# Reordered mixing stages, gate products moved into two projection units, and identity products between the steps of an encoder kernel

## What is computed

```python
def token_mixer(h, w_in, w_out, ...):
    proj = h @ w_in                                   # 1024 x 3088: 12 units of 256 or 512 columns and 16 gate columns
    p_ret, p_s5, p_hy, p_ml = jnp.split(proj, ...)
    y = jnp.concatenate([
        retention_mixer(p_ret, ...),   # rotary, 4 heads: scores * decay, then values, head norm
        s5_mixer(p_s5, ...),           # 16 groups of 64 complex states, forward and backward scan, GELU, gate
        hyena_mixer(p_hy, ...),        # short convolution, filters computed from w1..w3, 2 long convolutions by DFT
        mlstm_mixer(p_ml, ...)], -1)   # 4 heads, exponential gates, forward and backward, head norm
    return y @ w_out

def reference(x, ...):
    h = layer_norm(x, ...)
    for l in range(2):
        h = layer_norm(ALPHA * h + token_mixer(h, ...), ...)
        f = swiglu(h, ...) if l == 0 else moe_swiglu(h, ...)
        h = layer_norm(ALPHA * h + f, ...)
    return h
```

## Time and profile before

| | |
|---|---|
| median of 3 runs | 1711.05 us (1709.68 to 1712.01) |
| the profiled execution | 1715.15 us, its span 1713.3 us |
| mean granted clock of PE | 0.966 |
| busy: PE, DVE, ACT, POOL | 96%, 79%, 55%, 3% of the span |
| mixing stage 0 | 18.9 to 241.4 us |
| dense | 241.4 to 474.2 us |
| mixing stage 1 | 474.2 to 665.4 us |
| experts | 665.4 to 1713.3 us |

### The profile page before, as it was taken

How to read it: one execution, slowest core, us unless ns; L and a number is a source line. 1 busy time by engine, 2 the same in 40 slices (tenths; PEclk the granted TensorE clock), 3 DMA queues, 4 the chain that set the end, 5 groups by cost and what they waited for, 6 DMA issues and landing times.

```text
span 1713.3 us, 18404 instructions
## 1 busy us (share of the span) xinstructions
PE 1638.6 (96%) x7538; PEld 1278.9 (75%) x7538; DVE 1353.3 (79%) x1443; ACT 943.4 (55%) x941; POOL 56.5 (3%) x39
## 2 busy tenths in 40 slices
PE   6998989999999998899999999999999999999995
PEld 4555748988757665788888888888888888888883
DVE  6979456765666945688898888988989989888996
ACT  4312415644211231577776777777767767777772
POOL 0111000000011100000000000000000000000000
PEclk9999989999999988899999999999999999999997
DMA  7221152744433125598998998989989989989870
GB/s 313 98 98 49 74 213 98 271 172 154 185 134 142 49 81 240 200 377 340 370 355 344 368 359 339 360 347 360 365 347 356 360 339 369 362 329 374 351 300 26
DMA packets 40458, 444.21 MB, mean 259 GB/s; under 512 B 4400, under 2 KB 4528, under 8 KB 7216
## 3 DMA queue, kind: packets, MB, share of 16 engines
q1 hardware_dynamic: 39216, 438.78, 65.8%
q10 hardware_dynamic: 1152, 4.19, 0.6%
HBM read 437.71 MB, written 5.24 MB: 259 GB/s over the span
## 4 chain that ended last, share of the span: by engine, by line
PE 84%; DVE 11%; ACT 3%; issue 1%; DMA 0%; DVEq 0%; SPq 0%; ACTq 0%
PE bank L1062 34%; PE bank L1083 15%; PE bank L968 7%; PE bank L582 4%; PE bank L977 3%; PE bank L789 3%; PE bank L586 3%; PE bank L1026 2%; PE bank L1070 1%; PE bank L751 1%; DVE ring_lo L1943 1%; DVE ring_lo L2067 1%; ACT ex_up_hi L1334 1%; PE bank L1046 1%; PE bank L725 1%
## 5 line engine op out<-in xcount | busy, mean ns | idle before, releaser
L1943 DVE TENSOR_TENSOR ring_lo<-ring,ex_up_hi 128x2048 fp32r<-128x2048 f32 x224 | 513.0, 2290 | 50.9 <-ACT ex_up_hi L1334 50.7
L1334 ACT ACTIVATE ex_up_hi<-ring 128x2048 fp32r<-128x2048 f32 x224 | 429.1, 1916 | 115.9 <-PE bank L1062 108.2
L1062 PE MATMUL bank<-ex_up_hi,ex_x_hi 128*128 128x512 f32 x896 | 363.1, 405 | 3.7 <-DVE ring_lo L1943 3.7
L1062 PE MATMUL bank<-ring_lo,ex_x_hi 128*128 128x512 f32 x896 | 350.6, 391 | 0.0
L1062 PE MATMUL bank<-ex_up_hi,ex_x_lo 128*128 128x512 f32 x896 | 349.9, 390 | 0.0
L2067 DVE TENSOR_TENSOR ring_lo<-ring,ex_w_hi 128x2048 fp32r<-128x2048 f32 x112 | 255.6, 2282 | 1.4 <-ACT ex_w_hi L1430 1.4
L1430 ACT ACTIVATE ex_w_hi<-ring 128x2048 fp32r<-128x2048 f32 x112 | 213.2, 1904 | 0.0
L1062 PEld LDWEIGHTS bank<-ex_up_hi,ex_x_hi 128*128 128x128 f32 x896 | 168.3, 188 | 41.0 <-DVE ring_lo L1943 11.0
L1062 PEld LDWEIGHTS bank<-ring_lo,ex_x_hi 128*128 128x128 f32 x896 | 168.2, 188 | 36.1
L1062 PEld LDWEIGHTS bank<-ex_up_hi,ex_x_lo 128*128 128x128 f32 x896 | 168.8, 188 | 30.5
L1083 PE MATMUL bank<-ex_w_hi,ex_mid_hi 128*128 128x512 f32 x448 | 174.4, 389 | 2.1 <-DVE ex_mid_lo L2061 2.1
(11 more groups left out here) (313 smaller groups left out, 2140.5 us busy)
## 6 DMA issues: line engine op xcount, KB each, us to landing
ring<-moe SPq DMA_DIRECT2D x112, 2048.0 KB, 7.6
ring<-moe SPq DMA_DIRECT2D x112, 1024.0 KB, 7.4
ring<-ffn SPq DMA_DIRECT2D x11, 3072.0 KB, 10.9
win<-w_in SPq DMA_DIRECT2D x12, 2048.0 KB, 8.3
win<-w_out SPq DMA_DIRECT2D x4, 2048.0 KB, 10.3
lnb<-ln SPq DMA_DIRECT2D x4, 1024.0 KB, 6.6
tab<-yT ACTq DMA_DIRECT2D x8, 512.0 KB, 5.3
pr<-par SPq DMA_DIRECT2D x2, 1728.0 KB, 11.7
```

The lines of the kernel that those rows point to most:

```text
L1062: ins = mm(b[:, :], ex_x[x % 2][x_][:, k, :], (ex_up_hi, lo)[w_][:, k, :], start=(k == 0 and m == 0), stop=(k == KT - 1 and m == 2))
L1334: act(ex_up_hi[:, HS * q:HS * (q + 1), :], wt[:, HS * q:HS * (q + 1), :], ACT.Copy).then_inc(e_uh, 1)
L1943: tt(ring_lo[s][:, half], ring[s][:, half], hi.bitcast(F32), ALU.subtract).then_inc(e_ul, 1)
```

## The change

1. The gate products lose their unit. `unit` issues them for i = 8 and 9, one before each wide product on the same tokens, into bank 4 (columns 0 to 31). `UNITS` and `UNIT_BANK` have twelve entries, `pj` counts twelve units a layer, and `gates` waits for unit 9 and reads bank 4. In layer 1 unit 8 waits for one more spectrum to leave bank 4.
2. A new step on PE, `keep_busy(count, b)`: `count` products of the identity with itself, 128 x 128, into columns 384 to 511 of a bank; nothing reads them. They wait for nothing. Five calls in stage 0 (40 products), ten in stage 1 (68).
3. The lists `mix_0` and `mix_1` of PE, ACT and DVE stand in another order. No other piece of work is added or left out, and the lists of SP and POOL are the same but for the count of `pj`.

```diff
@@ -48,9 +48,9 @@
-UNITS = (0, 8, 9, 10, 11, 1, 2, 3, 12, 6, 7, 4, 5)
+UNITS = (0, 8, 9, 10, 11, 1, 2, 3, 6, 7, 4, 5)
...
-UNIT_BANK = (5, 6, 5, 6, 5, 6, 5, 6, 5, 6, 5, 1, 2)
+UNIT_BANK = (5, 6, 5, 6, 5, 6, 5, 6, 5, 6, 1, 2)
...
+            def keep_busy(count, b):
+
+                for _ in range(count):
+                    mm(bank[b][:, 384:512], ident, ident, start=True, stop=True)
...
-                elif i < 12:
+                else:
+                    with_gates = i in (8, 9)
+                    gw = W("gate_w").rearrange("p (k n) -> p k n", k=KT)
+                    if with_gates:
+                        pe.wait_ge(s_par, 16 * (l + 1))
+                        if l:
+                            pe.wait_ge(f_spec, 4 * l + 3)
                     for k in range(KT):
-                        ins = mm(b[:, :], hT[:, k, part * P:(part + 1) * P], w[:, k, :],
-                                 start=(k == 0), stop=(k == KT - 1))
-                else:
-                    gw = W("gate_w").rearrange("p (k n) -> p k n", k=KT)
-                    for t in range(TT):
-                        for k in range(KT):
-                            ins = mm(b[:, t * 16:(t + 1) * 16], hT[:, k, t * P:(t + 1) * P], gw[:, k, :],
-                                     start=(k == 0), stop=(k == KT - 1))
+                        x = hT[:, k, part * P:(part + 1) * P]
+                        if with_gates:
+                            mm(bank[4][:, part * 16:(part + 1) * 16], x, gw[:, k, :], start=(k == 0), stop=(k == KT - 1))
+                        ins = mm(b[:, :], x, w[:, k, :], start=(k == 0), stop=(k == KT - 1))
...
                 unit(0, 11)
+                pre(0, 0)
+                unit(0, 1)
+                pre(0, 1)
                 s5_in(0, 2)
-                unit(0, 1)
-                pre(0, 0)
                 unit(0, 2)
-                pre(0, 1)
...
+                keep_busy(8, 6)
                 ml_scores(1, 0)
                 out_product(1, "hyena", 3)
+                s5_glu(1)
+                keep_busy(8, 6)
                 head_out(2, 4)
-                s5_glu(1)
+                keep_busy(8, 6)
+                keep_busy(4, 6)
+                out_product(1, "s5", 3)
+                keep_busy(4, 6)
+                ml_scores(1, 1)
                 out_product(1, "ret", 3)
-                ml_scores(1, 1)
...
-                ve.wait_ge(pj, 13 * l + POS[12] + 1)
-                tt(gts, bank[UNIT_BANK[POS[12]]][:, 0:32].rearrange("p (t g) -> p t g", t=2), bc(W("gate_b"), 1, TT),
+                ve.wait_ge(pj, 12 * l + POS[9] + 1)
+                tt(gts, bank[4][:, 0:32].rearrange("p (t g) -> p t g", t=2), bc(W("gate_b"), 1, TT),
```

More of the change, by code:

```diff
@@ L572, in unit @@
                     pe.wait_ge(f_spec, 4 * l + p + 1)
-                j, part = next(((j, w[1].index(i)) for j, w in enumerate(WIN_LOADS) if i in w[1]), (None, 0))
-                if j is not None:
-                    s, v = win_use(l, j)
-                    pe.wait_ge(win_in[s], v)
-                    w = win[s][:, :].rearrange("p (k n) -> p k n", k=KT)
+                j, part = next((j, w[1].index(i)) for j, w in enumerate(WIN_LOADS) if i in w[1])
+                s, v = win_use(l, j)
+                pe.wait_ge(win_in[s], v)
+                w = win[s][:, :].rearrange("p (k n) -> p k n", k=KT)
                 if i < 6:
@@ L812, in mix_0 @@
                 pre(0, 3)
+                unit(0, 3)
+                pre(0, 4)
                 s5_y(0, 1)
-                pre(0, 4)
+                pre(0, 5)
                 s5_y(0, 2)
-                pre(0, 5)
-                s5_in(0, 4)
-                unit(0, 12)
                 unit(0, 6)
@@ L821, in mix_0 @@
                 s5_y(0, 3)
+                s5_in(0, 4)
+                pre(0, 7)
+                ml_gate_rows(0, 0)
+                pre(0, 8)
+                ml_gate_rows(0, 1)
+                pre(0, 9)
+                unit(0, 7)
+                pre(0, 10)
+                s5_y(0, 4)
                 s5_in(0, 5)
-                pre(0, 7)
-                pre(0, 8)
-                s5_y(0, 4)
+                hyena_transposes(0, 0)
+                hyena_forward(0, 0)
+                ml_columns(0)
@@ L826, in mix_0 @@
                 s5_in(0, 6)
-                pre(0, 9)
-                pre(0, 10)
-                ml_gate_rows(0, 0)
-                unit(0, 7)
-                hyena_transposes(0, 0)
-                ml_gate_rows(0, 1)
+                hyena_inverse(0, 0)
+                ret_transposes(0)
+                ret_scores(0, 0)
+                hyena_transposes(0, 1)
+                ret_scores(0, 1)
+                s5_y(0, 5)
+                ret_out(0, 0)
+                hyena_forward(0, 1)
@@ L895, in mix_1 @@
                 unit(1, 2)
-                s5_y(1, 0)
+                s5_y(1, 1)
                 unit(1, 3)
-                s5_y(1, 1)
-                unit(1, 12)
                 s5_y(1, 2)
+                ml_gate_rows(1, 0)
+                s5_y(1, 3)
                 hyena_transposes(1, 0)
-                s5_y(1, 3)
-                hyena_forward(1, 0)
-                ml_gate_rows(1, 0)
                 s5_y(1, 4)
@@ L907, in mix_1 @@
                 s5_in(1, 5)
+                hyena_forward(1, 0)
                 unit(1, 6)
                 hyena_inverse(1, 0)
+                s5_in(1, 6)
                 unit(1, 7)
@@ L1264, in mix_0 @@
                 pre(0, 15)
+                pre(0, 16)
                 take_unit(0, 8)
-                pre(0, 16)
                 pre(0, 17)
+                pre(0, 18)
                 take_unit(0, 9)
-                pre(0, 18)
+                pre(0, 19)
                 take_unit(0, 10)
-                pre(0, 19)
+                pre(0, 20)
                 take_unit(0, 11)
-                pre(0, 20)
+                pre(0, 0)
                 take_unit(0, 1)
-                pre(0, 0)
+                pre(0, 1)
                 take_unit(0, 2)
-                pre(0, 1)
+                pre(0, 3)
                 take_unit(0, 3)
-                pre(0, 3)
                 pre(0, 5)
@@ L1820, in mix_0 @@
                 pre(0, 16)
+                pre(0, 17)
                 s5_tile_products(0, 0)
-                pre(0, 17)
+                pre(0, 18)
                 s5_tile_scan(0, 0)
-                pre(0, 18)
+                pre(0, 19)
                 s5_tile_products(0, 1)
-                pre(0, 19)
+                pre(0, 20)
                 s5_tile_scan(0, 1)
-                pre(0, 20)
+                gates(0)
+                pre(0, 0)
+                pre(0, 1)
                 s5_tile_products(0, 2)
+                conv(0, 1)
                 s5_tile_scan(0, 2)
-                pre(0, 0)
-                conv(0, 1)
-                pre(0, 1)
+                pre(0, 2)
                 conv(0, 2)
-                pre(0, 2)
-                conv(0, 3)
                 pre(0, 3)
@@ L1889, in mix_1 @@
                 s5_tile_scan(1, 0)
+                gates(1)
                 s5_tile_products(1, 1)
```

169 lines of the change are left out of this document (82 added, 87 removed).

## The result

The changed kernel took 1715.21 us (median of 20 runs, 1712.50 to 1718.58), the kernel before, in 20 runs beside it, 1712.41 us (1709.57 to 1715.77): a ratio of 1.0016, 95% interval 1.0010 to 1.0023. By the prediction's bound of 0.2% that is no change, a little on the slow side. The prediction was 1705.5 us. In what follows a "filler" is an identity product, "none" stands for the change without any filler, and all window and timeline rows come from the one profiled execution of each kernel.

The account below looks back on a forecast made before the run. TensorE (PE) was taken to bound both mixing stages, losing time to waits and half clock. Stage 0 at -7.8 and stage 1 at +2.3 gave -5.5 us: 1709.7 from the profile, 1705.5 as median; range 1697 to 1716.

Parts of the forecast that it names:

- -7.8 and +2.3: Forecast changes in us of mixing stage 0 (233.6 against 241.4) and of mixing stage 1.
- For the clock I add 2 us: Mixing 0: one clock fall at the Hyena inverse and a chance of one between the L710 and L729 groups.
- The walk to the mLSTM part: Mixing 0: PE 9.1 us ahead early, last DVE scan ending at 169.8, first mLSTM scores at 187.5.
- case C: No change: fillers hold the clock, DVE's chain in stage 0 gives the lead back; 4 us worse, 1709.5; chance 0.22.
- C's sign: Stage 0: PE waits of over 10 us would show that DVE's chain gives the lead back.
- Added: 68 fillers, 136 x 0.11 = 15.0: Stage 1: filler instructions cost 0.11 us each, 15.0 us together, nearly all in line, not in waits.
- Gone, if the clock holds: 14.2: Stage 1: 14.2 us of waits and half clock vanish from 191.17, leaving 177 at full clock.
- 0.6 of small waits: Stage 1: small waits add 0.6 us, beside 0.9 for the uncovered evacuation.
- The base: Whole kernel before: median 1711.05 us, 4.1 below the profiled 1715.15; the forecast takes the same step down.
- Rival E: Gate products nearly free, as next weights load under a running product; better, 1698.5 us; chance 0.06.
- B: Slower: fillers don't hold the clock; mLSTM stretches of both stages run partly at 1.2 GHz; 20 more, 1725; chance 0.14.
- D: Better: a third of the fillers' 24 us stands in waits not seen beforehand; 1697.5 us; chance 0.08.

## Why the prediction was wrong

**Its mechanism held, several of its sizes did not.** Fillers do hold the clock (in mixing 1 throughout, in mixing 0 it fell once among them), the gate products between wide ones cost 0.10 an instruction, the order of mixing 0 gives a lead. The forecast was -7.8 and +2.3; the profile shows -4.1 and +4.4. The 9.7 us between 1705.5 and 1715.21 are 3.8 in mixing 0, 2.1 in mixing 1, less 0.6 in the other stages, 1.4 in the base, and 3.1 that no stage shows.

**Mixing 0, "For the clock I add 2 us".** This is the largest of the terms that failed there. The walk to the mLSTM part was made at full clock, and 2 us were laid on its end. The trace has three stretches of half clock of some 3.4 us each (137 to 142, 148 to 152, 199 to 203). The first ends in PE's wait for L1675 and costs little; the two others cost 1.7 each, 3.4 for the 2 that were set. The other terms are smaller:

- Unit 4, said to be done before the last scan ends, is done at 172.7, 2 us behind it, and the first scores come 2.9 us late (190.4 for 187.5). 1.7 of that is the half clock at 148 to 152, 0.4 the price of 16 fillers (3.9 us for 3.5). The other 0.8 must lie ahead of 147.22, where PE waits for the slowed L1675: from there to 190.4 it never waits again, so that the scan's end, 0.9 late, is not on its path.
- Behind the first scores the list took 47.0 us, where 44.1 and the 2 for the clock were set: 1.7 of half clock at 199, 0.2 more for the 24 fillers, and some 1.0 in the output products and the last stretch.

In time this is case C (4 us worse in this stage), to which I gave 0.22, but not by its cause: PE waited 8.0 us in all, where C's sign was over 10, and GpSimd's add held DVE once (1.3 us at L1675, where the walk had 1 for it), not in two places more.

**Mixing 1, "Added: 68 fillers, 136 x 0.11 = 15.0" and "Gone, if the clock holds: 14.2".** The fillers took 16.0, since the pair of transposes that the price came from the earlier trace rows stood between wide products, and a run of sixteen takes 0.118 each. In all 216 instructions that is 1.7 us. And 14.2 was too much to regain: at full clock PE is busy 194.47 us, without the fillers' 16.0 that is 178.5, and the walk had 177. The stage before was busy 188.08 us, so its half clock cost 9.6, its waits 3.1, together 12.7. Against that, only 0.1 of the "0.6 of small waits" came.

**The base.** The sum was set on the median of three runs, 1711.05. The next 20 runs of the same kernel gave 1712.41 (later groups 1713.37, 1714.01 and 1713.46), so 1.4 us of the miss were in the base and not in the change. The 3.1 left are the 2.7 us by which the profiled execution of before lay above that median, and the 0.3 by which the other lay below its own; in which stages they are stays open.

**What was not asked.** The prediction's own sum had fillers at 24 us (3.5 + 5.3 + 15.0) and never set them against what they hold. In stage 1 it found 14.2 us to be regained and 15.0 to be paid, and went on to the total. The same rows would have told that the order without fillers is the version to build: 9.4 + 16.0 us paid, for at most 6.8 us of lost time in mixing 1 and 3.4 in mixing 0 (17.1 us of half clock without, in the worse draw, 10.2 with). This, more than any single size, is why nothing was gained: without its fillers the change is 0.7 to 1.1% faster than before. Rival E, gate products nearly free, falls (8.75 us for unit 8); B falls too, since the clock in mixing 1 was 1.00; D falls, since by the runs without fillers only 1.8 us of real waits stood in mixing 1 (0.80 and 1.02) to hide 16.0.

**The two rules cited.** At 199 to 201 PE is busy 1.00 of each window and the clock is 0.67, then 0.50. The Trainium skill (TensorE: Matmul & The Clock Gate, Part 1: the HAM clock gate) ties the half rate to an idle engine; the trace disagrees, as in the earlier trace rows. Unit 8 took 8.75 us for a unit of 7.1 and sixteen gate instructions, 0.10 each. By the Trainium skill (TensorE: Matmul & The Clock Gate, Part 2: What happens when you issue a matmul), where the next weights load under a running product, they could have been free; the trace disagrees with that reading of it.

## What to carry to other kernels

Price a clock filler both ways: n instructions in line at their measured step against half of the half-clock time that it ends; here 0.118 us each, and 25 us of them bought at most 10 and some 2 us of waits. Put wide work that must be done anyway between the small products first; here that held the clock in one stage in three kernels, at no instruction more. A filler came cheap only in a wait of the engine that bounds (1.5 us shorter in one profile); where another engine sets the pace most of what it saved was waited away at the next step. And with a reordering that carries fillers, time it once without them. What makes the clock fall, and why one kernel draws differently each time, these runs don't show.

## What the runs showed that was not expected

- The clock can fall inside a run of 128-column identity products with PE never idle (0.50 at 200 us in mixing 0), though 68 or 136 such instructions elsewhere kept mixing 1 at 1.00.
- One kernel draws different amounts of half clock: 10.2 and 3.4 us at the same place in two executions, 3.75 us of mixing 0, and medians of the same code at 1696.35 (4 runs) and 1699.58 (6 runs, another chip). The kernel before repeats its mixing stages within 0.5 us.
- A small group takes exactly double at half clock, as a wide one does, if the clock is at 0.50 for all of it: twelve 65-column instructions (L725 in before) take 2.75 us from 208.96 to the next start, 1.39 at full clock, a wide output product 3.6 and 1.8. The 1.9 to 2.1 us that L729 shows above are groups in which the clock changes.
- A product on DVE beside one of GpSimd's adds took 2.03 us, without it 0.69 (L1675 here and in both profiles of none, L1658 before). The reorder put the two side by side.
